# Issuing the key/value cache copies from GpSimd instead of SyncE in a two-layer decoder step

## What is computed

```python
h = x + W_out(concat[A(xn), B(xn), C(xn)])      # xn = RMSNorm(x), one input projection W_in
# A: windowed softmax attention, three groups (window, dilation) = (128,1), (512,4), (2048,16)
# B: gated causal convolution of width 3;  C: chunked spatial gating
y = h + PEER(RMSNorm(h))                         # 8 heads, 16 of 16384 single-neuron experts each
```

```python
kv_all = jnp.concatenate([kv_buf, kv_new], axis=1)   # per group: the old rows, then 4 new ones
return o, lse, kv_all[:, -lb:]                       # the last lb rows: 128, 512 or 2048
```

## Time and profile before

| | us |
|---|---|
| median of 3 runs | 1824.12 |
| lowest and highest | 1823.39, 1826.02 |
| the profiled execution, its own time | 1825.49 |
| its span, from the first to the last instruction | 1823.5 |
| PE busy | 1553.7 (85%) |
| DVE busy | 1110.1 (61%) |
| POOL busy | 706.9 (39%) |
| ACT busy | 605.2 (33%) |

### The profile page before, as it was taken

The page is one execution under the profiler, slowest core; times in us unless marked ns, Lnnn a source line. Parts: engine busy times, 40 slices in busy tenths (PEclk is TensorE's granted clock), DMA queues, the critical chain, the costliest instruction groups (busy, mean ns, idle before and its releaser), DMA issues.

```text
span 1823.5 us, 18407 instructions
## 1 busy us (share of the span) xinstructions
PE 1553.7 (85%) x5776; PEld 837.7 (46%) x5776; DVE 1110.1 (61%) x2782; ACT 605.2 (33%) x1873; POOL 706.9 (39%) x682
## 2 busy tenths in 40 slices
PE   8999997999888777788689998979888887877777
PEld 5789644554333332233147895545443333322221
DVE  3445665666888775454535367565868878654444
ACT  2332432333343332222333334233333333322222
POOL 5111453544544443234313024534464444433341
PEclk9999999999998999899889999989998889999999
DMA  9889999999999999999979999999999999999997
GB/s 335 338 360 359 404 414 421 373 421 421 421 420 422 421 421 421 422 422 421 421 284 385 370 363 389 415 387 421 421 421 421 421 421 422 421 421 421 422 421 308
DMA packets 102838, 730.03 MB, mean 400 GB/s; under 512 B 14993, under 2 KB 16114, under 8 KB 21972
## 3 DMA queue, kind: packets, MB, share of 16 engines
q0 software_dynamic: 90432, 627.75, 83.6%
q1 hardware_dynamic: 11760, 100.48, 13.8%
q10 hardware_dynamic: 548, 0.62, 0.1%
HBM read 724.54 MB, written 48.10 MB: 424 GB/s over the span
## 4 chain that ended last, share of the span: by engine, by line
PE 42%; DMA 41%; DVE 10%; ACT 3%; issue 2%; DVEq 2%; ACTq 1%; SPq 0%
DMA arena<-peer_uv,idx 22%; PE bank L1758 20%; DMA wring<-peer_uv,idx 11%; PE bank L1515 7%; PE bank L1682 4%; DMA qf<-peer_uv,idx 4%; PE bank L1722 3%; DVE arena L1339 3%; DVE wring L1339 2%; DMA arena<-peer_wq 2%; PE bank L1510 1%; DMA yt<-peer_uv,idx 1%; ACT diag L863 1%; DVE route L1311 1%; PE bank L1592 1%
## 5 line engine op out<-in xcount | busy, mean ns | idle before, releaser
L1758 PE MATMUL bank<-arena,diag 128*128 128x512 f32 (+1 forms) x1416 | 664.8, 613 | 109.0 <-ACT diag L863 109.0
L1339 DVE SCALAR_TENSOR_TENSOR arena<-arena,xn 128x1024 f32<-128x1024 f32 x378 | 458.3, 1225 | 327.5 <-DMA arena<-peer_uv,idx 326.3
L640 POOL DMA_INDIRECT arena<-peer_uv,idx x378 | 415.4, 1099 | 597.8 <-PE bank L1758 444.6
L1758 PEld LDWEIGHTS bank<-arena,diag 128*128 128x128 f32 (+1 forms) x1416 | 261.4, 190 | 468.2 <-issue 290.7
L855 ACT ACTIVATE act<-hid 128x2 f32<-128x2 f32 x287 | 58.4, 204 | 907.2 <-DVE arena L1339 597.6
L863 ACT ACTIVATE diag<-ident,weight 128x128 f32<-128x128 f32 (+1 forms) x574 | 194.3, 385 | 20.9 <-issue 1.4
L1758 PE MATMUL bank<-wring,diag 128*128 128x512 f32 x336 | 164.5, 629 | 39.8 <-ACT diag L863 39.8
L640 POOL DMA_INDIRECT wring<-peer_uv,idx x84 | 98.5, 1172 | 130.1 <-PE bank L1758 120.7
L1758 PE MATMUL bank<-qf,diag 128*128 128x512 f32 (+1 forms) x216 | 113.4, 665 | 40.7 <-ACT diag L863 40.7
L1339 DVE SCALAR_TENSOR_TENSOR wring<-wring,xn 128x1024 f32<-128x1024 f32 x84 | 102.3, 1225 | 74.0 <-DMA wring<-peer_uv,idx 73.2
L858 ACT ACTIVATE weight<-act,gate 128x1 f32<-128x1 f32 x574 | 138.0, 287 | 19.8
(11 more groups left out here) (289 smaller groups left out, 1577.6 us busy)
## 6 DMA issues: line engine op xcount, KB each, us to landing
kvs<-cache_a_kv_w SPq DMA_DIRECT2D x32, 1022.0 KB, 10.4
wring<-w_col SPq DMA_DIRECT2D x15, 1024.0 KB, 8.6
wring<-w_tok SPq DMA_DIRECT2D x8, 1408.0 KB, 8.5
arena<-peer_wq SPq DMA_DIRECT2D x10, 1024.0 KB, 14.0
kvs<-cache_a_kv_w SPq DMA_DIRECT2D x16, 508.0 KB, 11.8
arena<-peer_uv,idx POOLq DMA_INDIRECT x378, 20.6
qf<-cache_keys POOLq DMA_DIRECT2D x8, 576.0 KB, 10.8
qf<-cache_values POOLq DMA_DIRECT2D x8, 576.0 KB, 20.3
```

The costliest lines, as they stand in the source:

```text
L640: pool.indirect_dma_start(out=ring[j], out_offset=None, in_=io["peer_uv"], in_offset=bass.IndirectOffsetOnAxis(ap=idx[:, n:n + 1], axis=0) ...
L1339: last = v.scalar_tensor_tensor(out=ring[j][:, 0:D], in0=ring[j][:, 0:D], scalar=1.0, in1=xn[:, i, :], op0=ALU.mult, op1=ALU.mult, accum_o ...
L1758: last = pe.matmul(bank[b0 + half][0:r, :], diag[:, n % 16, 0:r], ring[SLOT_OF[n]][:, D + 512 * half:D + 512 * half + 512], start=False, s ...
```

## The change

`shift` moves from the program of SP to that of POOL and is otherwise the same. A new helper on POOL, `shifts_after`, waits for an input chunk to be done and then issues copies. SP keeps the weights alone.

```diff
-                    for m in range(3 * (c - 2) // 2, 3 * (c - 1) // 2 if c < N_IN else 17):
-                        shift(l, m)
                 sp.wait_ge(probt_ps, 3 * (l + 1))
                 load_o(l, 2)
                 sp.wait_ge(pv_done, 2 * (l + 1))
                 load_o(l, 1)
-                for m in range(17, 19):
-                    shift(l, m)
...
                 load_q(l, 0)
-                shift(l, 19)
...
                 load_q(l, 1)
-                for m in range(20, 24):
-                    shift(l, m)
                 for chunk in (2, 4, 5):
                     load_q(l, chunk)
...
+            def shifts_after(l, chunk, first, end):
+
+                pool.wait_ge(in_ps, len(OUTS) * l + IN_DONE[chunk])
+                for m in range(first, end):
+                    shift(l, m)
...
+                shifts_after(l, 0, 0, 1)
+                shifts_after(l, 1, 1, 3)
+                shifts_after(l, 2, 3, 4)
+                shifts_after(l, 3, 4, 6)
+                shifts_after(l, 4, 6, 7)
                 pool.wait_ge(qk_done, 6 * (l + 1))
                 pool.memset(pz, 0.0).then_inc(pz_clear, 1)
...
                     load_v(l, KEY_ORDER[n])
+                    if n == 4:
+                        shifts_after(l, 5, 7, 9)
                 pool.wait_ge(key_ps, NB * (l + 1))
                 load_v(l, 0)
+                shifts_after(l, 6, 9, 10)
...
+                shifts_after(l, 7, 10, 12)
+                shifts_after(l, 8, 12, 13)
+                shifts_after(l, 9, 13, 15)
+                shifts_after(l, 10, 15, 19)
                 pool.wait_ge(conv_kept, l + 1)
                 pool.dma_start(io["conv_rows"][l, 0:2 * P].rearrange("(c p) j -> p c j", p=P), crt[:, 0:2, :]).then_inc(rows_out, 16)
                 pool.dma_start(io["conv_rows"][l, 2 * P:BW], crt[0:64, 2, :]).then_inc(rows_out, 16)
 
+                shift(l, 19)
+                pool.wait_ge(h_ps, 16 * l + 1)
+                for m in range(20, 24):
+                    shift(l, m)
                 pool.wait_ge(rows_out, 16 * N_ROWS * (l + 1))
```

More of the change, by code:

```diff
@@ L466, in load_o @@
                 sp.dma_start(wo_home(chunk), io["w_out"][l, chunk]).then_inc(wo_loaded[chunk - 1], 16)
[L468 to L479, removed]
             load_w(0, 0)
@@ L499, in _ @@
                 for c in range(2, N_IN + 1):
-                    if l and c == HELD:
-                        sp.wait_ge(in_ps, len(OUTS) * l + IN_DONE[0])
-                    else:
+                    if not l or c != HELD:
                         sp.wait_ge(in_ps, len(OUTS) * l + IN_DONE[0 if l and c == HELD + 2 else c - 2])
                         load_w(l, c)
-                    for m in range(3 * (c - 2) // 2, 3 * (c - 1) // 2 if c < N_IN else 17):
-                        shift(l, m)
                 sp.wait_ge(probt_ps, 3 * (l + 1))
@@ L563, in _, with shift @@
                                                   ap=[[PITCH - 1, P], [P * PITCH, HEADS], [1, 2 * P]])).then_inc(toep_loaded, 16)
+            def shift(l, m):
+                b, part = m // 3, m % 3
+                for (win, _), src, dst, rows in zip(GROUPS, ("cache_a_kv_w128", "cache_a_kv_w512", "cache_a_kv_w2048"),
+                                                    ("kvs128", "kvs512", "kvs2048"), (16, 64, 256)):
+                    if (win == 2048) == (part == 2):
+                        continue
+                    d_ = io[dst].rearrange("l b r k h d -> l b (r k h d)")[l, b, 0:(win - NT) * 256].rearrange("(q n) -> q n", q=rows)
+                    s_ = io[src].rearrange("l b r k h d -> l b (r k h d)")[l, b, NT * 256:win * 256].rearrange("(q n) -> q n", q=rows)
+                    if win == 2048:
+                        d_, s_ = d_[P * part:P * part + P], s_[P * part:P * part + P]
+                    pool.dma_start(d_, s_).then_inc(shift_out, 16)
             def load_k(l, b):
                 pool.dma_start(kc[b], io["cache_keys"][l, b]).then_inc(k_in[b], 16)
+            def shifts_after(l, chunk, first, end):
+                pool.wait_ge(in_ps, len(OUTS) * l + IN_DONE[chunk])
+                for m in range(first, end):
+                    shift(l, m)
             def load_v(l, b):
```

## The result

The changed kernel takes 1866.94 us, median of 4 runs (1860.1 to 1867.7), beside 1824.3 for the kernel before on the same chip: +42.6 us, a ratio of 1.0229 with a 95% interval of 1.0216 to 1.0242. I had said 1848, between 1828 and 1858. The sign and the kind of cause were right, the size was not.

The account below looks back on a forecast made before the run. It took PE's chain to bound the mixer stages and DMA engines the gathers. 2.5 + 8.9 - 3.3 + 2.7 + 9.1 + 3.8 = +23.7 us on 1825.5 gave 1849.2, stated as 1848 us; range 1828 to 1858.

Parts of the forecast that it names:

- the frame: Whole kernel: a mixer stage lasts as long as PE's chain; late weights add to its end, copies matter only through weights.
- the rhythm of the tail: Tail of layer 0: without copy 0 of layer 1 the last dot products keep a steady rhythm, -3.3 us.
- turns of one packet against one row: Both queues: they alternate by packet, 64 KB of copy against 8 KB of weight, so waiting copies precede a load's last row.
- who is there first: Mixer stages: a copy overtakes the load issued with it; copies 4 and 5 bring chunk 5 of layer 0 to 74.3.
- Rival 3: Both queues: turns of whole transfers, so no stand at the mixer's end; +1.9 us, 1826 us, chance 0.09.
- copy 0 against chunk 2 alone: Start of layer 0: the copy costs nothing or 2.5 us; taken as 0, with today's wait of 2.0.
- the end of the mixer stage, layer 0: Copies 19 to 23 overtake chunk 0 of `peer_wq`, landing at 161.3 us; PE stands +8.9 us.
- Layer 1 is alike: End of the mixer stage, layer 1: `peer_wq` lands at 1058.7, needed at 1049.61, +9.1 us.
- My sign: First query product, both layers: PE waits 7 us or more for `peer_wq`, with a clock near 0.5 behind it.
- BS, layer 1: Input projection, layer 1: chunk 6 plus copy 6 comes at 978.7, BS begins at 976.03, +2.7 us.
- BS, layer 0: Input projection, layer 0: copy 6 overtakes chunk 6, lateness of chunk 5 lies inside, +2.5 us in all.
- The clock: Behind the two stands of 9 us: products at about half clock, +3.8 us for two; none after shorter BS waits.

Follow-up runs that it names:

- e7b: The changed kernel with short batches of products of no use ahead of PE's stands for weights; 1864.22 us, ratio 1.0210.
- e13: e11 with copy 0 of layer 1 issued behind copies 20 to 23 of that layer; 1821.74 us, ratio 0.9988.
- e14: The changed kernel with copies 20 to 23 of each layer held until the seventh product group of the output projection; 1853.19 us, ratio 1.0165.
- e3: The changed kernel with copies 19 to 23 of each layer back on SP at their old places; 1848.07 us, ratio 1.0132.
- e9: The changed kernel with copies 19 to 23 of both layers left out; 1845.09 us, ratio 1.0120.
- e6: The kernel before with only copies 19 to 23 of each layer moved to POOL; 1838.13 us, ratio 1.0085.
- e5: The changed kernel with copies 0 to 3 of layer 1 back on SP in their old places; 1855.19 us, ratio 1.0171.
- e11: e6 with copies 20 to 23 held until the seventh product group of the output projection, not the first; 1823.27 us, ratio 1.0002.

## Why the prediction was wrong

**Right: the frame.** The copies matter only through the weights, and what a weight is late in a mixer stage is added to the end. The gather stages are the same length within 2.5 us. Right too that SP's issue time is worth nothing, that POOL's 32 issues cost nothing, and that copies on q0 are cut into packets of 64 KB: from 55 to 63 us the changed kernel has 34 packets on q0 for 1.08 MB.

**Right: the rhythm of the tail. Its size is not shown.** I said -3.3 us and a steady rhythm. The last groups of 8 products start at 934.46, 939.42, 944.35 and 949.30, each after a wait of 1.7 us, and the wait of 4.05 is gone. The whole part comes out shorter by 1.5 only. The slow clock behind the last stand of layer 0 lies at its beginning and costs 2.7 there (e7b), which would hide most of the gain; e13, which takes the same copy away, gained 1.9.

**Half right: turns of one packet against one row.** The turns are as I took them: 144 packets against 146, 176 against 176, 284 against 286. What failed is what I built on them, that every copy waiting at an engine goes before a load's last row because no group has more than 7 packets. I left out the 4-byte completions, which take a turn each: copies 15 to 19 and copies 20 to 23 are 6 transfers and so 12 packets each at an engine, and a load's 9 turns let through 4 or 5 transfers. That is a little milder for a single load than I said. But it goes on for as long as copies are there, and it meets every load, the next one behind it in the same queue too. I looked for loads that are overtaken, found one at chunk 6 and one at the end of each layer, and called the rest covered.

**Failed: who is there first.** I let a copy overtake the load that is issued with it. But where SP had just issued a load, the first row of a POOL copy moved 3.7 to 4.2 us after its issue (55.51 to 59.2, 66.61 to 70.8, 133.63 to 137.4), and the load had 7 or 8 of its 8 rows at each engine through by then. With no load beside it, it took 1.2 us (968.87 to 970.1). So chunk 5 of layer 0 lost one turn to copies 4 and 5, not both copies, and landed in 8.6 us where it had 6.5. The harm is done to the load that comes when copies are under way already, as chunk 1 of `w_out` and chunk 5 of layer 1 show.

The Trainium skill (DMA: Bandwidth & Descriptors, Queues, rings and completion order) has an engine drain a packet of some 9 to 17 descriptors before it goes to another queue. By that a load's 8 rows and completion would go in one piece. For the load that is there first this would fit. From 139 to 142.5 us it does not: each engine moved two rows of weight between one packet of 64 KB and the next. If a row is one descriptor, this case does not bear the rule out for these turns. Rival 3, which came from it, gave 1826 us and is out.

**Failed: a stand that is in no term, layer 0 (+2.1 us).** At 57.32 us PE stands 2.1 us for `w_col`, chunk 3 of the input projection, which landed in 13.9 us instead of 6.8. Copies 0 to 2 are beside it. I had looked at copy 0 against chunk 2 alone, and there it cost nothing, 2.2 us for 2.0. A stand for `w_col` between 50 and 75 us is in eight of the ten profiles that have these copies on POOL, 1.4 to 2.4 us long, and in none of the seven that have them on SP (the versions with 8 KB pieces left aside).

**Failed: the end of the mixer stage, layer 0 (+8.9 us), in its cause.** The stands add up to 9.9 us, so the sum looks right. But 6.0 of them are at chunk 1 of `w_out`, of which I wrote that it is late by about 1 us and that this "lies inside". It is made by copies 15 to 19, as e14, e3 and e9 show together; copies 17 to 19 stood behind that chunk before. Copies 20 to 23, to which I gave all but 2.5, come too late for chunk 0 of `peer_wq` when they are alone on POOL (e6: no stand there). Their victim is chunk 3 of `w_out`, of which I wrote that it adds nothing. In the changed kernel all of them pile up, and the last stand, 3.9 us, is at `peer_wq`. Layer 1 is alike: 9.1 said, 2.2 + 8.1 measured. My sign, a wait of 7 us or more at the first query product in both layers, came in layer 1 alone. That the two sums come out within 1.2 us is luck.

**Failed: BS, layer 1 (+2.7 us).** "Copies 0 to 3 are bunched behind the keys, but their 9 us are over by about the time of chunk 5." They were issued from 968.87 on, and chunk 5 at 975.38; they were not over, as q1 moved nothing until 980.5. PE stood 8.5 us, and e5 gives the group 10 to 12 us in all. This is the largest single miss, and the two times could have been set side by side before: POOL's wait for the last gather (935.60) and its keys against SP's own issues.

**BS, layer 0: +2.5 us said.** The stand grew from 0.5 to 2.0. By the first product of chunk 7 the changed kernel is 5.8 us late (90.72 for 84.97), of which this stand accounts for 1.5 more than before and the stands for `w_col` for 2.3 more; the clock behind them (0.91 from 80 to 100 us) is a part of the rest.

**The clock: +3.8 us.** Products behind stands run at half speed, as I took from the earlier trace rows, and there are more stands than I had: the granted clock is 0.78 from 160 to 180 us and 0.74 from 980 to 1000, where before it was 1.00 in both. What of it reaches the end is open. The spans differ by 41.6 us and the stands by 34.4. That leaves 7 us, or up to 10.5 if the tail gave back its 3.3, for the clock and for scatter, while e7b, 2.7 us below the changed kernel, can't be told from it.

```profile
160.00:180.00 20.00, 16.09 (x110) 15.90 (x110) 3.88 (x15) 1.55 (x5) 0.00 (x0) 0.78 0.95 390
...
980.00:1000.00 20.00, 11.46 (x87) 7.68 (x88) 4.96 (x5) 1.96 (x6) 0.49 (x1) 0.74 0.72 282
```

The first row answers to the earlier trace rows: where the engines idled at 0.72 before, they still work at 0.95, as the copies and weights of the end come 17 us later.

**The size in one sentence:** I had 23.7 us, and of the 17.9 that are missing up to the 41.6 between the spans, 5.8 are the stand behind the bunch ahead of chunk 5 of layer 1, 4.2 the stands for `w_col` that were in no term (2.3 in layer 0, 1.9 in layer 1), 1.2 what the other stands come out above their terms, and 6.7 the clock, the tail and scatter, for which I had 0.5 together.

## What to carry to other kernels

A second queue for background copies does not free the weights. It gives up the order that put a copy behind the weight issued with it, and hands the copies turns of their own just when a weight is due: here, with 64 KB against 8 KB in a turn, three quarters of the engines' time. If copies go to another queue, they need a wait of their own that puts them where no load is due (e11: 15 us back for one changed constant), and it must be checked what they are bunched with when their engine comes out of a long wait. Large merged packets on the competing queue are dear, here down to 32 KB.

## What the runs showed of the hardware

- Two queues with work at the same time moved their packets one for one, the 4-byte completions counted: 144 to 146, 176 to 176 and 284 to 286 with copies in packets of 64, 32 and 16 KB against rows of 8 KB. The queue with the small rows so had 23, 30 and 40% of the time of the 16 engines, and 51% against gathers in rows of 8 KB.
- Copies in packets of 16, 32 and 64 KB cost 10, 36 and 43 us over the same copies on SP. Why the step between 16 and 32 KB is the large one stays open, and so does why 8 KB costs more over its control (23 us) than 16 KB.
- A transfer that comes to engines at work for the other queue does not get its turn at once. POOL's copies had their first row 1.2 us after the issue with q1 idle (968.87 to 970.1 us in the changed kernel), and 3.7 to 4.2 us after it beside a load that had just been issued (55.51, 66.61 and 133.63 us). Only then did the turns go one for one. Why the first turn is longer is open.
- Copies within the device's memory in strided pieces of 8 KB filled the engines at 256 to 328 GB/s, and cost 83 us on SP's queue; strided pieces of 16 KB cost 3 us, of 32 KB 1 us or nothing. Why 8 KB is so much dearer was not found.
